# Rows p, 128+p, 256+p of w_in in partition p, and one set of transposes of x for projections, residual and router

## What is computed

```python
h = rmsnorm(x, norm_mix)                     # x * rsqrt(mean(x*x)) * norm_mix
u, q, k, v, f_logit, g_logit = split(h @ w_in)          # w_in: 1024 x 4104
x = x + (sig(g0) * (pool(u) @ w_up_pool) + sig(g1) * (attention(q, k, v, logf) @ w_up_att)) @ w_out
x = x + hier_moe(rmsnorm(x, norm_ffn))       # router, 32 experts of 1024 x 512, top 2 of one group of 8
y = rmsnorm(x, norm_final)
```

## Time and profile before

| | us |
|---|---|
| median of 3 runs | 713.96 |
| lowest and highest | 713.72 and 715.38 |
| the profiled execution: its own time | 713.79 |
| its span in the profile | 712.0 |
| PE busy | 592.1 (83%) |
| PE weight loads busy | 380.3 (53%) |
| DVE busy | 219.1 (31%) |
| ACT busy | 86.1 (12%) |
| POOL busy | 52.5 (7%) |
| bytes moved by DMA | 269.17 MB, 378 GB/s over the span |

### The profile page before, as it was taken

One profiled execution on the slowest core, in us unless ns is written; L12 is line 12 of the kernel. 1 busy time (PEld: TensorE's weight loads), 2 busy tenths in 40 slices (PEclk: granted clock), 3 DMA queues, 4 the chain that ended last, 5 costly groups with the idle time before them and its releaser, 6 DMA issues.

```text
span 712.0 us, 13756 instructions
## 1 busy us (share of the span) xinstructions
PE 592.1 (83%) x6139; PEld 380.3 (53%) x6139; DVE 219.1 (31%) x538; ACT 86.1 (12%) x231; POOL 52.5 (7%) x58
## 2 busy tenths in 40 slices
PE   9999899999899999999676787667777768776793
PEld 7778687775488865455333344333444334443441
DVE  4159996982141253212111111111111111111113
ACT  3311233320000150000000000000000000000012
POOL 5126421122000000000000000000000000000000
PEclk9999999999999999999889789897889887898898
DMA  9985989997999869999999999999999999999991
GB/s 294 305 315 215 339 152 423 367 381 304 402 414 412 358 250 425 424 425 424 424 424 421 428 425 425 423 422 427 426 424 423 424 423 426 424 423 421 409 371 77
DMA packets 42403, 269.17 MB, mean 378 GB/s; under 512 B 9844, under 2 KB 10672, under 8 KB 23903
## 3 DMA queue, kind: packets, MB, share of 16 engines
q1 hardware_dynamic: 29984, 229.34, 80.1%
q0 software_dynamic: 3072, 35.19, 12.1%
q10 hardware_dynamic: 9287, 3.74, 2.0%
HBM read 266.02 MB, written 2.46 MB: 377 GB/s over the span
## 4 chain that ended last, share of the span: by engine, by line
DMA 61%; PE 21%; issue 6%; DVE 6%; ACT 2%; POOL 2%; SPq 0%; POOLq 0%; DVEq 0%; ACTq 0%
DMA ring<-w_up 48%; DMA x<-w_up 6%; PE bank L1652 4%; PE bank L1638 3%; PE bank L1379 3%; DVE ring L1041 3%; DMA ring<-cache_v,ridx 2%; DMA ring<-cache_k,ridx 2%; DMA front<-q_scratch 1%; DMA q_scratch<-x 1%; PE bank L1569 1%; PE bank L1488 1%; PE bank L1592 1%; PE bank L1479 1%; PE bank L1395 1%
## 5 line engine op out<-in xcount | busy, mean ns | idle before, releaser
L1379 PE MATMUL bank<-ring,front 128*32 128x256 f32 x1856 | 158.5, 479 | 87.8 <-DMA ring<-w_up 75.2
L1379 PEld LDWEIGHTS bank<-ring,front 128*32 128x32 f32 x1856 | 84.3, 137 | 147.0 <-issue 123.2
L1241 DVE COPY front<-bank 128x256 f32<-128x256 f32 x32 | 13.6, 425 | 232.4 <-PE bank L1379 232.4
L1592 PE MATMUL bank<-hT,ring 128*128 128x264 f32 x256 | 59.8, 389 | 2.4 <-DMA ring<-w_in 2.0
L1395 PE MATMUL bank<-ring,front 128*32 128x256 f32 x928 | 55.4, 379 | 0.0
L1592 PEld LDWEIGHTS bank<-hT,ring 128*128 128x128 f32 x256 | 47.7, 190 | 12.1 <-DMA ring<-w_in 2.4
L867 ACT ACTIVATE front<-bank 128x128 f32<-128x128 f32 x32 | 8.9, 277 | 370.4 <-PE bank L1387 370.4
L1363 PE MATMUL bank<-front 128*32 128x256 f32 (+1 forms) x768 | 52.3, 385 | 0.3 <-DVE front L1141 0.3
L1497 PE MATMUL bank<-hT,ring 128*128 128x264 f32 x192 | 44.5, 388 | 0.0
L1395 PEld LDWEIGHTS bank<-ring,front 128*32 128x32 f32 x928 | 30.0, 110 | 20.7 <-issue 1.1
L1251 DVE COPY front<-bank 128x256 f32<-128x256 f32 x32 | 13.6, 425 | 88.0 <-PE bank L1395 88.0
(11 more groups left out here) (311 smaller groups left out, 561.9 us busy)
## 6 DMA issues: line engine op xcount, KB each, us to landing
ring<-w_gate SPq DMA_DIRECT2D x28, 2048.0 KB, 14.7
ring<-w_up SPq DMA_DIRECT2D x28, 2048.0 KB, 14.7
ring<-w_down SPq DMA_DIRECT2D x28, 2048.0 KB, 14.7
ring<-w_in SPq DMA_DIRECT2D x8, 2048.0 KB, 22.9
x<-w_gate SPq DMA_DIRECT2D x3, 2048.0 KB, 14.7
x<-w_up SPq DMA_DIRECT2D x3, 2048.0 KB, 14.7
x<-w_down SPq DMA_DIRECT2D x3, 2048.0 KB, 15.4
ring<-w_out SPq DMA_DIRECT2D x2, 2048.0 KB, 20.4
```

The lines of the kernel that those rows point to most:

```text
L1241: v.tensor_copy(gu.rearrange("p (c n) -> p c n", c=2), bank[GATEUP][:, 0:QUART].rearrange("p (n c) -> p c n", c=2)).then_inc(s_gusb, 1)
L1379: last = m.matmul(bank[GATEUP][32 * g:32 * g + 32, 0:256], xgT[:, k % 2, k // 2], w[:, k, 256 * (g % 2):256 * (g % 2) + 256], start=k == 0 ...
L1592: last = m.matmul(out[:, 0:TOK], w[:, k, cols], hT[:, k, 0:TOK], start=k == 0, stop=k == DK - 1)
```

## The change

w_in's rows are laid out in plain chunks (partition p of chunk k holds row 128k+p), in the blocks of SyncE as in wf, and norm_mix goes the same way. With that, the projections want the same transposes of x as the residual and the router. The transposes with a step of 8 become plain ones, the second set goes, and ScalarE copies xT out of the banks from which VectorE also makes hT, each pair after VectorE has read it, and after it has issued the late loads. The samples' columns of xT are copied by VectorE ahead of L957. The banks change (XBANK is now PART, SUM, QB, CHAIN; the samples' go to SCORES, the roots to TR). Behind the spread roots TensorE runs 12 matmuls of the identity into BIG0 whose result nobody reads. TensorE's wait for s_xraw and for the last chunk of hT stand ahead of L1488.

```diff
-        XBANK = (BIG0, BIG1, SCORES, TR)
-        RAWX = (PART, SUM, QB, CHAIN)
+        XBANK = (PART, SUM, QB, CHAIN)
...
                     sp.dma_start(dst.rearrange("p (k n) -> p k n", k=DK // 2),
-                                 w_in[:, C_Q * DC:C_Q * DC + D].rearrange("(p k) n -> p k n", p=P)[:, ks]).then_inc(done, 16)
+                                 w_in[:, C_Q * DC:C_Q * DC + D].rearrange("(k p) n -> p k n", p=P)[:, ks]).then_inc(done, 16)
                 elif kind in "wg":
                     first = W_GATE + a * DC if kind == "g" else a * DC
-                    sp.dma_start(dst.rearrange("p (k n) -> p k n", k=DK), w_in[:, first:first + DC].rearrange("(p k) n -> p k n", p=P)).then_inc(done, 16)
+                    sp.dma_start(dst.rearrange("p (k n) -> p k n", k=DK), w_in[:, first:first + DC].rearrange("(k p) n -> p k n", p=P)).then_inc(done, 16)
...
-            act.dma_start(nmix[:], t["norm_mix"][0].rearrange("(p k) -> p k", p=P)).then_inc(in_nm, 16)
+            act.dma_start(nmix[:], t["norm_mix"][0].rearrange("(k p) -> p k", p=P), allow_slow_non_contiguous=True).then_inc(in_nm, 16)
...
-            act.dma_start(wf[:, :, 0:HEADS], w_in[:, W_FORGET:W_FORGET + HEADS].rearrange("(p k) n -> p k n", p=P)).then_inc(in_wf, 16)
+            act.dma_start(wf[:, :, 0:HEADS], w_in[:, W_FORGET:W_FORGET + HEADS].rearrange("(k p) n -> p k n", p=P)).then_inc(in_wf, 16)
...
-            s.copy(rootB, bank[CHAIN][:, 0:TOK]).then_inc(s_rootB, 1)
-            for i in range(DK // 2):
-                act.wait_ge(s_x2, i + 1)
-                s.copy(xT[:, 2 * i:2 * i + 2, 0:SEQ], bank[RAWX[i]].rearrange("p (k n) -> p k n", k=2)).then_inc(s_xraw, 1)
+            s.copy(rootB, bank[TR][:, 0:TOK]).then_inc(s_rootB, 1)
...
             late_loads()
-            act.wait_ge(s_x2, DK // 2 + 1)
-            s.copy(xT[:, :, SEQ:TOK], bank[SUM][:, 0:DK * NS].rearrange("p (k t) -> p k t", k=DK)).then_inc(s_xraw, 1)
+            for i in range(DK // 2):
+                act.wait_ge(s_hT, 2 * i + 3)
+                s.copy(xT[:, 2 * i:2 * i + 2, 0:SEQ], bank[XBANK[i]].rearrange("p (k n) -> p k n", k=2)).then_inc(s_xraw, 1)
...
             dve.wait_ge(in_nm, 16)
             dve.wait_ge(s_xTs, 1)
-            link(v.tensor_tensor(hT[:, :, SEQ:TOK], bank[QB][:, 0:DK * NS].rearrange("p (k t) -> p k t", k=DK),
+            v.tensor_copy(xT[:, :, SEQ:TOK], bank[SCORES][:, 0:DK * NS].rearrange("p (k t) -> p k t", k=DK))
+            link(v.tensor_tensor(hT[:, :, SEQ:TOK], bank[SCORES][:, 0:DK * NS].rearrange("p (k t) -> p k t", k=DK),
...
-                        dve.wait_ge(s_xraw, DK // 2 + 1)
+                        dve.wait_ge(s_xraw, DK // 2)
...
-            xk = x[:].rearrange("t b (p k) -> t b k p", k=DK)
             for i in range(DK // 2):
+                if i == 1:
+                    pe.wait_ge(s_ridx, 1)
                 for k in (2 * i, 2 * i + 1):
                     for b in range(PB):
-                        last = m.transpose(bank[XBANK[i]][:, (k % 2) * SEQ + b * P:(k % 2) * SEQ + (b + 1) * P], xk[:, b, k], ident)
+                        last = m.transpose(bank[XBANK[i]][:, (k % 2) * SEQ + b * P:(k % 2) * SEQ + (b + 1) * P], x[:, b, k * P:(k + 1) * P], ident)
                 last.then_inc(s_xT, 1)
             pe.wait_ge(in_xs, 16)
             for k in range(DK):
-                last = m.transpose(bank[QB][:, k * NS:(k + 1) * NS], xk[0:NS, 2, k], ident8)
+                last = m.transpose(bank[SCORES][:, k * NS:(k + 1) * NS], x[0:NS, 2, k * P:(k + 1) * P], ident8)
             last.then_inc(s_xTs, 1)
...
-                last = m.matmul(bank[CHAIN][:, b * P:b * P + n], ones[0:n], diag[0:n, b, 0:n], start=True, stop=True)
+                last = m.matmul(bank[TR][:, b * P:b * P + n], ones[0:n], diag[0:n, b, 0:n], start=True, stop=True)
             last.then_inc(s_rB, 1)
-            for i in range(DK // 2):
-                if i == 1:
-                    pe.wait_ge(s_ridx, 1)
-                elif i == 2:
-                    pe.wait_ge(s_hT, 1)
-                elif i == 3:
-                    pe.wait_ge(s_rootB, 1)
-                for c in (2 * i, 2 * i + 1):
-                    for b in range(PB):
-                        last = m.transpose(bank[RAWX[i]][:, (c % 2) * SEQ + b * P:(c % 2) * SEQ + (b + 1) * P], x[:, b, c * P:(c + 1) * P], ident)
-                last.then_inc(s_x2, 1)
+            for _ in range(12):
+                m.matmul(bank[BIG0][:, 0:P], ident, ident, start=True, stop=True)
...
+                            pe.wait_ge(s_hT, DK + 1)
                             pe.wait_ge(s_xraw, DK // 2)
-                            for c in range(DK):
-                                last = m.transpose(bank[SUM][:, c * NS:(c + 1) * NS], x[0:NS, 2, c * P:(c + 1) * P], ident8)
-                            last.then_inc(s_x2, 1)
-                            pe.wait_ge(s_hT, DK + 1)
```

More of the change, by code:

```diff
@@ L420, in build @@
         s_h2, s_xsq, s_xsum, s_nat = (sem(n) for n in ("rows_normalised", "chunk_squared", "chunk_squares_added", "residual_rows_turned"))
-        s_x2, s_xraw, s_sums, s_roots = (sem(n) for n in ("raw_x_transposed", "raw_x_copied", "square_sums_copied", "roots_ready"))
+        s_xraw, s_sums, s_roots = (sem(n) for n in ("raw_x_copied", "square_sums_copied", "roots_ready"))
         s_fin2, s_rsum = sem("second_block_ready"), sem("row_squares_summed")
```

## The result

The changed kernel takes 720.67 us (median of four executions), the kernel before beside it 714.67. One of the four, 729.57, was disturbed and is left out of the ratio; without it the median is 719.17. The ratio is 1.0067 [1.0038, 1.0095]. Run again later (a1, the same kernel) the median was 720.90 and the ratio 1.0092 [1.0055, 1.0130]. So the change makes the kernel slower by 0.7 to 0.9%, 4.8 to 6.6 us; the forecast was 2.7 us. The profiled execution took 718.64 us, span 716.8, which is 4.8 over the span of before.

What follows compares the result with a forecast made beforehand. The DMA-full end was taken as pinned to TensorE and VectorE work before 264 us. L1479 3.5 us late, less 0.59 for L1482 and 0.24 slack, gave 2.7: 713.79 + 2.7 = 716.5 us, range 713.9 to 719.0.

Steps and rivals of the forecast that it cites:

- What bounds the kernel: DMA is full at the end, but TensorE and VectorE work before 264 us sets when that stretch starts.
- The scales: Head: nmix, now 1024 runs of 4 B, lands at about 16.7 us, not 6.4; L1479 starts at 18.3.
- The one-for-one counts: Head queues: q10's packets keep q1's pace, 555 + 490 = 1045 by 16.4 us, covering nmix's 1024.
- What 3 us of late start are worth: Second halves of the q projection start 2.9 us late; after 0.24 us slack, 2.7 us reach the end.
- Rival D: Behind 74 us the delay is partly absorbed by a later, faster K gather: 714.0 to 715.5 us; chance 0.12.
- The clock in the new wait: TensorE idles from 15.7 to 18.3, 2.6 us; the forecast costed no clock fall there.
- rival B: The clock falls in TensorE's new wait in the head, costing 1.7 us of matmul time: 718.2 us; chance 0.27.
- The layout of the big weights: nothing.: Loads of w_in and wf: new row order, same runs and number, costed at zero.
- E: w_in's loads take 11% less in the new order, shrinking the K gather's wait: 709 to 711.6 us; chance 0.04.
- The hand-over at L1022: VectorE waits for ScalarE's copy of the last k projection with 0.24 us slack, so 2.7 us arrive there.
- The merged transposes, the copies, wf: Head: removed transposes, added matmuls and moved copies hide under waits or L1479, except L1482's 0.59 us gain; wf costs zero.

Runs made afterwards that it cites:

- e2: The kernel before with only norm_mix read in the new order (1024 runs of 4 B): ratio 1.0040, median 715.87 us.
- e4: The kernel before with TensorE held up by 15 unused matmuls ahead of its second transposes: ratio 1.0041, median 715.79 us.
- e23: The changed kernel with late scales and merged transposes kept, but w_in and the forget weights in the old row order: ratio 1.0070.
- e18: The changed kernel with the two router bias loads put ahead of the router's weight loads: ratio 1.0057.
- e12: The changed kernel with GpSimd's wait for and scaling of the router weights moved from before the K gathers to step m1: ratio 1.0278.
- e19: The kernel before with the new row order only in the loads of the projections' and forget weights: ratio 0.9997.
- e14: The changed kernel with the old row order of w_in, forget weights and scales, leaving only merged transposes and moved copies: ratio 1.0002.
- e10: The changed kernel with TensorE kept busy by extra identity matmuls in its three idle waits: ratio 1.0115, median 723.18 us.
- e13: The kernel before with GpSimd's wait for and scaling of the router weights moved from before the K gathers to step m1: ratio 1.0224.
- e3: The kernel before with the new row order alone, in all loads of w_in and the forget weights: ratio 1.0074, median 720.37 us.
- e15: The kernel before with the new row order in the four gate-weight loads alone: ratio 1.0048.
- e1: The changed kernel with norm_mix loaded as before (128 runs of 32 B), so the scales are early: ratio 1.0086.
- e7: The changed kernel with the scales loaded as eight rows of 512 B and turned by TensorE: ratio 1.0052, median 716.82 us.
- e22: The changed kernel with scales loaded as eight rows and turned by TensorE, and router bias loads ahead of the router's weights: ratio 1.0032.
- e17: The kernel before with the two router bias loads put ahead of the router's weight loads: ratio 0.9982.
- e11: The kernel before with identity matmuls filling TensorE's waits at the forget gates' transposes (7) and gate 0 (9): ratio 0.9990.
- e9: The changed kernel with scales turned by TensorE and ScalarE's router loads moved forward, behind the last rows of u: ratio 1.0051.

## Why the prediction was wrong in size and right in direction

It said slower, 716.5 us, at most 719.0; measured were 720.7 and, the second time, 720.9. Point by point:

- **What bounds the kernel** held. The end followed the work in front of 264 us one for one: last V gather +5.2, first expert matmul +5.2, hole +5.2, span +4.8; and the constant distance from the hole's last load to the end holds in all twenty profiles.
- **The scales** landed at 17.13 against 16.7, and L1469 started at 18.70 against 18.3. The one-for-one counts held from 10 to 16.4 us (455 to 458). Before, from 4 to 10 us, q10 passed 866 packets to q1's 531. So it had passed 1321 by 16.4 us where I had added up 1045, more than the scales' 1024, and they still landed only at 17.13. The sum isn't how the landing comes about, and its near hit is partly luck. The Trainium skill, "DMA: Bandwidth & Descriptors", section "Queues, rings and completion order", has an engine drain a packet of typically 9 to 17 descriptors from one queue before it turns; the measured 1.0 to 1.6 tiny ones per large one fit turns of like numbers from both queues, and speak against reading it as relief.
- **What 3 us of late start are worth**: 1.0040 and 1.0041, 2.9 us, against 2.7, in the kernel before. The number is right by luck: the hand-over that it was read from isn't the one (below), and e2's start of the gate loads is twice as late as e4's for the same 2.9.
- **Rival D**, with 0.12: its mechanism came. A K gather that goes out later takes less time: in e4 108.97 for 103.94 and 10.38 us for 13.19, so that VectorE's product of it is 2.2 us late and not 5.0; in a1 7.5 us late at its issue and 4.0 at the product. It didn't in e23 (5.1 and 5.2). The forecast let its 2.7 us arrive there whole.
- **The clock in the new wait**: the forecast took no fall, rival B a price of 1.7 us. B's mechanism came in four of the six profiles of kernels with late scales and an unfilled wait (a1, e18 and e23: 32 matmuls at 8.87, 9.04 and 10.31 us, 1.5 to 2.95 over 7.36; e2: clock 0.66), not in e12, and in the first profile of after it came at the next wait, behind 1.65 us of idling. I had set the forecast apart from B by the length of the idling, 2.6 us between 2.33 without a fall and 3.06 with one. That length doesn't decide: the clock fell after 2.70, 3.87, 4.28 and 4.40 us and not after 3.10 and 3.63. By this count B deserved more than its 0.27. Its 718.2 is still short of 720.7, and its price at the end is not shown.
- **The layout of the big weights: nothing.** This is the step that failed most. In the projections' loads it was right within the interval (e19 0.9997). In the gates' loads the new order costs 3.4 us (1.0048), in all loads 5.3 us (1.0074), and with all row orders old the changed kernel is back at 1.0002 (e14). I had a rival for a faster row order (E, from the 11% between the earlier trace rows) and none for a slower one, though zero was a choice between unlike rows and both signs were open. The range ended at 719.0 for want of it.
- **The hand-over at L1022.** I read the copy at 73.05 in the earlier trace rows as the last k projection's. It is one of v; the last one of k is at 65.05, and the small copy behind it ends at 65.50, so VectorE had 8.2 us of slack there and not 0.24, and the step came 0.10 us late and not 2.7. The delay travelled by another way that I hadn't looked at: TensorE's last k projection frees the place of the first gate load (65.04 to 70.05), gate 0 starts 3.6 us late, and the router's loads on ScalarE follow it (91.98 to 95.60).
- **ScalarE's issues**, absent from the prediction. The router's loads go out near the start of a gate load. In the kernel before their issue takes about 7 us in all; with more in the queues one issue takes 2.07 (after) or 8.73 (e10), or four 20.50 us (e13), and ScalarE's copies and TensorE wait behind it. The change's loss doesn't need it: in a1, the same kernel, the issue of 2.07 us takes 0.48, and TensorE has no such wait. The Trainium skill, "Perfetto Trace Analysis", section "What "DMA-bound" means", reads the time of an issuing instruction as descriptor generation; the same load at 0.60 and at 8.73 us shows that the state of the queues is in it as well.

```profile
101.14 0.48 ACTq L744 DMA_DIRECT2D blocks<-b_router_group  x1
```

- **Do the costs add?** Not settled. Late scales alone are 1.0040 (e2) or 1.0070 (e23), the row order alone 1.0074 (e3), both together 1.0067 and 1.0092. The sum with e2, 1.0114, lies in the interval of the second and not of the first, the sum with e23, 1.0144, in neither.
- **The merged transposes, the copies, wf**: cost nothing measurable, as costed (e14 1.0002 [0.9980, 1.0024]; wf landed 23.6 us after its issue, with no wait).

**What stays open.** How the new row order of the gates' loads costs 3.4 us (5.3 with all loads new). The profiles show the way of a delay but not this size. In twelve of the twenty the chain of waits runs through the K gather behind GpSimd's wait for the router, and the last V gather goes out 56.8 us after VectorE's product of that gather. With the new order and early scales (e3, e15, e1, e7, e22) this product starts at 117.97 to 119.44 us, as here in e3,

```profile
119.06 1.23 DVE L1041 TENSOR_TENSOR ring<-ring,part 128x1024 f32<-128x1024 f32 x1 [6.93 <-DMA ring<-cache_k,ridx]
```

against 117.15 before and 115.70 to 117.66 in e14, e17 and e19, whose gate loads are old. But e11, with all loads old, has 120.61, so single executions differ as much. And behind the V gather the profiles of e3 and e1 lose 1.5 and 2.3 us more than before's, where the clock fell (a window of e3, then one of e1; the kernel before has 1.00 in both):

```profile
190.00:200.00 10.00, 7.80 (x49) 4.23 (x48) 1.21 (x4) 0.58 (x1) 0.00 (x0) 0.83 1.03 395
```

```profile
260.00:264.00 4.00, 4.00 (x26) 1.99 (x22) 1.96 (x9) 1.66 (x2) 0.00 (x0) 0.50 0.82 339
```

Such falls stand in e9's profile (new order) and e23's (old) too, so nothing ties them to the row order. e17 and e18 don't confirm the router's wait as its way. The profiled executions of e3 and e15 lie 3 us under their kernels' medians; that of e1, 718.49, is its kernel's median.

One idea is in the Trainium skill, "DMA: Bandwidth & Descriptors", section "Latency and other measured facts": copies slow down at row pitches of large powers of two from partition to partition, and a pad of 4 KiB gives the rate back. Here it is the neighbouring pieces within a partition that lie 128 rows of 16416 B apart in the new order, 2 MiB and 4 KiB. If the rule held for them, the pad would save it; the shares of q1 show a small loss all the same, and no run here varied the pitch.

## What to carry to other kernels

A change of a load's row order is no free edit even where runs, count and bytes stay the same: give it a price with both signs, and try it alone first (here 0 us were forecast and 5.3 measured). Before a delay is followed through the trace, find for each load which engine's last use frees its place, and read DMA-issuing instructions on a compute engine as work that stretches with what else is in the queues. Ask at each gather on the way whether it takes less time when it goes out later: 5.0 us late at the issue were 2.2 at its use in e4. A wait that looks like a loss, as GpSimd's for the router's weights, may be what keeps other transfers away.

## What the runs showed of the hardware that was not expected

- 1024 runs of 4 B land 15.7 to 16.9 us after their issue beside a large load (six profiles), where 128 runs of 32 B take 5.0.
- The issue of the load of the router's expert biases (128 runs) on ScalarE takes from 0.35 (e9) to 8.73 us (e10); that of the four loads of 1024 runs from 3.11 (e18) to 20.50 (e13).
- The granted clock fell after idle waits of TensorE of 1.65, 2.20 and 2.70 us in some executions (after, e3, e18), and stayed up after 3.10 and 3.63 us in others (after, e12).
- Loads of 2 MB of the same rows in another order over the partitions: the kernel takes 0.5% more where they stand beside small loads and gathers (e15), nothing measurable at the head (e19).
- A gather of keys that goes out 5.0 us later lands 2.2 us later (e4), 7.5 us later 4.0 (a1), but 5.1 us later 5.2 (e23).
